# Output projection of an encoder: row blocks 8 to 11 kept in split form on chip and multiplied last, tile by tile

## The chip, the core and the metric

The kernel runs on one core of a Trainium2 chip, in one launch. The metric is the device time of that launch in microseconds (us). TensorE (PE in the profile, PEld for its weight loads), VectorE (DVE), ScalarE (ACT), GpSimd (POOL) and the queue of SyncE (SP), which issues all the DMAs here, each run their own list of instructions in order and meet only at semaphores.

## What is computed

Two encoder layers over 1024 tokens of 1024 values. Each layer projects its input to queries, keys, values and a gate, attends, and closes with the output projection and a LayerNorm. The change is in that closing part and in what surrounds it:

```python
D_MODEL = 1024; SEQ = 1024; DEPTH = 2; D_INNER = 2 * D_MODEL
for i in range(DEPTH):
    ...
    y = jnp.concatenate([o_mix, o_mem], axis=1).transpose(0, 2, 1, 3).reshape(b, L, D_INNER)
    y = y * jax.nn.silu(gate)
    branch = jnp.einsum('ble,ed->bld', y, w_out[i])
    x = layer_norm(ALPHA * x + branch, ln_g[i], ln_b[i])
```

## The kernel before

All matmuls are made in three parts. An operand is split into a high part (a cast by ACT, `split_hi`, `y_tile`) and a low part (source minus high part, by DVE, `split_lo`, `y_tile`), and PE adds high by high, high by low and low by high.

**Output projection.** The 2048 values of `y` are 16 row blocks e of 128. The 1024 tokens are two halves h of 512, each of 4 row tiles t of 128 tokens. For one half the output is 4 tiles by 2 column halves c: 8 PSUM banks b = 2t + c, all of them. A block therefore costs 8 x 3 = 24 matmuls of 128x512, and a layer 2 x 16 x 24 = 768. PE goes through the blocks outside and the banks inside; only the last two blocks of a half are interleaved (`last_two`, lead 5). All eight banks of a half so end close together.

**Supply.** SP loads each weight piece (128x512, a *stage*) of `w_out` into `raw` (6 places) and each half block of `y` from `y_scratch` into `y_raw` (2 places). ACT and DVE split weights into `ring` (4 places, so two blocks) and `y` into `y_split` (2 places). A place is free when PE has ended the last matmul that reads it. In the order of the program all of them are 3 stages ahead of PE (`AHEAD`). Every weight piece is loaded and split twice, once for each half. The queue of SP also loads the residual rows (8 DMAs of 512 KB, one with each of the blocks 4 to 11 of the first half), `ln_g` and `ln_b`.

**After the matmuls.** DVE adds a bank to the residual (`add`), takes statistics for a tile (`statistics`), POOL turns them into a reciprocal deviation by four small operations, and `norm` scales and shifts: for tiles 0 to 3 DVE normalises and multiplies and POOL adds `b_row` over 1024 columns; for tiles 4 to 7 ACT normalises (L1521) and DVE does two operations of 1024 columns. Tiles 0 to 3 are normalised during blocks 4 to 7 of the second half, tiles 4 to 7 after its end. When layer 0 is closed, the rows are turned to columns for layer 1: `x_group` is four PE transposes (L1063) into a bank, a cast by ACT (L1306) and a subtraction by DVE; group 0 comes from the rows, others from sums of rows (`token_sums` and three more, DVE). Product 0 of layer 1 (12 matmuls) needs all four pieces of group 0, product 1 needs group 1, and PE transposes group 2 ahead of product 1.

## Time and profile before

| | us |
|---|---|
| median of 3 runs | 2169.07 (2167.77 to 2170.2) |
| the profiled execution, its own time | 2170.46 |
| its span, first to last instruction | 2168.6 |
| PE busy in the span | 2107.2 (97%) |
| DVE busy | 1628.4 (75%) |
| ACT busy | 1091.1 (50%) |
| mean granted TensorE clock | 0.99 |

PE is busy for 97% of the span, so a change can only win where PE stands still, or lose by making it do so. The page shows the span in 40 slices of 54 us; only slice 16 (813 to 867 us, the passage from layer 0 to layer 1: PE 5 tenths) and the last one are far from full. The output projections lie at 646 to 826 us and at 1973 to 2151 us.

### The profile page before, as it was taken

To read this page: it belongs to the slowest core of one execution; us is meant where nothing else is said; L and a number is where in the kernel's file an instruction comes from. 1 tells how busy PE (TensorE), PEld (TensorE's weight loads), DVE (VectorE), ACT (ScalarE), POOL (GpSimd) and SP (SyncE) were. 2 spreads that over 40 slices of the span, in tenths; PEclk is the share of its full clock that TensorE was granted. 3 is DMA by queue.
4 is the path that set the end of the run, shared out by engine and by line. 5 is a ranking of instruction groups with operands and counts; after the bars stand their busy time and mean duration, and the time that the engine had idled before them with its cause. 6 is when DMAs were issued, how large, how long until landed. Compare 5 with 4: busy or idle time off the path is not lost.

```text
span 2168.6 us, 31853 instructions
## 1 busy us (share of the span) xinstructions
PE 2107.2 (97%) x10880; PEld 1767.9 (82%) x10880; DVE 1628.4 (75%) x3673; ACT 1091.1 (50%) x2649; POOL 48.4 (2%) x65
## 2 busy tenths in 40 slices
PE   8999999999999995999999999999999999999996
PEld 8888888888888774888888888888888888888875
DVE  6777878787663568868888888888887888775485
ACT  5444444445553323455555555555555565564332
POOL 0000000000000021000000000000000000000031
PEclk9999999999999997999999999999999999999998
DMA  8311111111126542123233133133143233224643
GB/s 266 103 48 42 60 39 49 59 59 59 54 80 216 182 141 102 54 69 94 63 97 93 56 100 95 50 108 99 50 108 86 63 108 85 89 87 161 216 142 131
DMA packets 244619, 209.20 MB, mean 96 GB/s; under 512 B 21092, under 2 KB 198316, under 8 KB 244460
## 3 DMA queue, kind: packets, MB, share of 16 engines
q1 hardware_dynamic: 244460, 207.16, 31.8%
q8 instruction: 89, 1.46, 0.3%
q14 instruction: 70, 0.57, 0.1%
HBM read 172.60 MB, written 34.52 MB: 96 GB/s over the span
## 4 chain that ended last, share of the span: by engine, by line
PE 78%; DVE 13%; DMA 5%; issue 2%; ACT 2%; SPq 0%; DVEq 0%; ACTq 0%
PE bank L1086 15%; PE bank L1084 15%; PE bank L1085 15%; PE bank L1162 8%; PE bank L1134 7%; DVE work L1536 5%; PE bank L1256 4%; PE bank L1260 4%; PE bank L1262 4%; PE bank L1148 4%; DVE ring L1536 2%; DMA work<-weight_scratch 1%; DMA weight_scratch<-trig 1%; DVE x_ops L1536 1%; PE bank L1063 1%
## 5 line engine op out<-in xcount | busy, mean ns | idle before, releaser
L1084 PE MATMUL bank<-x_ops,ring 128*128 128x512 f32 (+1 forms) x1808 | 844.5, 467 | 16.9 <-issue 14.8
L1086 PE MATMUL bank<-x_ops,ring 128*128 128x512 f32 (+1 forms) x1808 | 698.9, 387 | 0.0
L1085 PE MATMUL bank<-x_ops,ring 128*128 128x512 f32 (+1 forms) x1808 | 697.0, 386 | 0.0
L1536 DVE SCALAR_TENSOR_TENSOR ring<-raw,ring 128x512 fp32r<-128x512 f32 x400 | 272.9, 684 | 232.9 <-ACT ring L1302 232.6
L1086 PEld LDWEIGHTS bank<-x_ops,ring 128*128 128x128 f32 x1808 | 341.0, 189 | 71.3
L1084 PEld LDWEIGHTS bank<-x_ops,ring 128*128 128x128 f32 x1808 | 345.7, 191 | 61.4 <-issue 15.5
L1363 ACT COPY work<-bank 128x256 f32<-128x256 f32 (+2 forms) x448 | 164.3, 367 | 430.1 <-PE bank L1148 429.3
L1085 PEld LDWEIGHTS bank<-x_ops,ring 128*128 128x128 f32 x1808 | 345.5, 191 | 37.5
L1302 ACT CAST ring<-raw 128x512 fp32r<-128x512 f32 x400 | 246.5, 618 | 198.4 <-PE bank L1262 173.0
L1162 PEld LDWEIGHTS bank<-work 128*128 128x128 f32 x1744 | 262.2, 190 | 44.4 <-ACT work L1363 3.9
L1380 ACT ACTIVATE work<-work,soft 128x256 f32<-128x256 f32 (+2 forms) x448 | 226.5, 506 | 134.3 <-DVE soft L1680 132.6
L1134 PE MATMUL bank<-work 128*128 128x256 f32 (+2 forms) x896 | 267.2, 380 | 3.0 <-DVE soft L1680 3.0
L1162 PE MATMUL bank<-work 128*128 128x128 f32 x1744 | 267.6, 275 | 2.5 <-ACT work L1363 1.2
L1536 DVE SCALAR_TENSOR_TENSOR work<-work 128x512 f32<-128x512 f32 (+4 forms) x352 | 233.3, 678 | 34.5 <-DMA work<-weight_scratch 31.5
L1134 PEld LDWEIGHTS bank<-work 128*128 128x128 f32 x896 | 183.3, 215 | 39.9 <-DVE soft L1680 7.8
L1536 DVE SCALAR_TENSOR_TENSOR work<-work,trig 32x512 f32<-32x512 f32 x304 | 207.2, 710 | 0.8
L1256 PE MATMUL bank<-ring,x_ops 128*128 128x512 f32 x512 | 200.4, 391 | 6.9 <-DVE x_ops L1536 5.3
L1262 PE MATMUL bank<-ring,x_ops 128*128 128x512 f32 x512 | 199.3, 389 | 0.0
L1260 PE MATMUL bank<-ring,x_ops 128*128 128x512 f32 x512 | 199.3, 389 | 0.0
L1536 DVE SCALAR_TENSOR_TENSOR ring<-sums,ring 128x512 fp32r<-128x512 f32 x180 | 123.0, 683 | 68.2 <-ACT ring L1302 68.1
L1148 PE MATMUL bank<-ident,work 128*128 128x128 f32 x872 | 168.7, 273 | 0.5 <-DVE work L1690 0.5
L1148 PEld LDWEIGHTS bank<-ident,work 128*128 128x128 f32 x872 | 114.2, 140 | 34.9 <-ACT work L1380 4.5
(74 smaller groups left out, 2020.8 us busy)
## 6 DMA issues: line engine op xcount, KB each, us to landing
raw<-in_w_in_b SPq DMA_DIRECT2D x160, 256.0 KB, 3.1
raw<-in_w_out SPq DMA_DIRECT2D x128, 256.0 KB, 2.9
raw<-in_w_in_a SPq DMA_DIRECT2D x80, 256.0 KB, 3.0
work<-weight_scratch SPq DMA_DIRECT2D x24, 768.0 KB, 5.2
y_scratch<-work SPq DMA_DIRECT2D x32, 512.0 KB, 2.8
x_ops<-y_scratch SPq DMA_DIRECT2D x64, 256.0 KB, 3.7
work<-v_scratch SPq DMA_DIRECT2D x48, 256.0 KB, 4.4
raw<-in_w_mkv SPq DMA_DIRECT2D x32, 256.0 KB, 5.1
```

The lines of the kernel that those rows point to most:

```text
L1084: nc.tensor.matmul(dst, w_h, x_h, start=start, stop=False, skip_group_check=again)
L1085: nc.tensor.matmul(dst, w_h, x_l, start=False, stop=False, skip_group_check=again)
L1086: return nc.tensor.matmul(dst, w_l, x_h, start=False, stop=stop, skip_group_check=again)
L1134: nc.tensor.matmul(SB[count % 2][:, 0:size], q, k, start=True, stop=True).then_inc(s_ready, 1)
L1148: mm = nc.tensor.transpose(TB[x_n % 2][:, c * P:(c + 1) * P], p[:, k0:k0 + P], ident[:, :])
L1162: mm = nc.tensor.matmul(dst, job.values(v), pT[layer][count % 2][:, c * P:(c + 1) * P], start=(c == 0), stop=(c == len(chunks) - 1))
L1256: mm = nc.tensor.matmul(BB[b][:, :], y_h, ring[:, n % RING, 0, :], start=first, stop=False)
L1260: nc.tensor.matmul(BB[b][:, :], y_h, ring[:, n % RING, 1, :], start=False, stop=False)
L1262: mm = nc.tensor.matmul(BB[b][:, :], y_l, ring[:, n % RING, 0, :], start=False, stop=last)
L1302: nc.scalar.copy(ring[:, n % RING, 0, :], src).then_inc(w_hi, 1)
L1380: nc.scalar.activation(p_view(layer, count % 3, size, sink), s_view(layer, count % 3, size, sink), ACT.Exp, bias=low[:, job.stat, t:t + 1] ...
L1536: return nc.vector.scalar_tensor_tensor(out=dst, in0=a, scalar=1.0, in1=b, op0=ALU.mult, op1=op)
```

## The change

Row blocks 8 to 11 are called LATE, the other twelve EARLY; the *place* of an early block is its index among these. In the first half, after the stages of the early blocks at places 1, 4, 7 and 10, the two weight stages of one late block are loaded and split, not into the ring but into `late`, and stay there for both halves. The `y` of the late blocks goes to four more places of `y_split`, in both halves. Stages of a layer fall from 64 to 56. PE multiplies the early blocks as before and the late ones at the end of a half, tile by tile: for tile 0 all four late blocks, then tile 1, and so on. `add` and `statistics` stand together for each tile. In the second half `norm` of tiles 4 to 6 stands between them, and in layer 0 group 0 of the columns and the first sums of rows do too. The bigger `y_split` and `late` take memory that products 2 to 5 of the last pair read, so the first two loads of `y` wait for product 3 and not for product 2. Residual rows are loaded at places 5 to 8 of the first half and at places 1 to 4 of the second, `ln_g` and `ln_b` at places 10 and 11.

```diff
-OUT_STAGES = 4 * NE
+
+
+EARLY = (0, 1, 2, 3, 4, 5, 6, 7, 12, 13, 14, 15)
+LATE = (8, 9, 10, 11)
+
+
+
+OUT_ORDER = []
+for half in range(2):
+    for place, block in enumerate(EARLY):
+        OUT_ORDER += [(half, block, 0), (half, block, 1)]
+        if half == 0 and place % 3 == 1:
+            OUT_ORDER += [(0, LATE[place // 3], 0), (0, LATE[place // 3], 1)]
+OUT_STAGES = len(OUT_ORDER)
+Y_ORDER = [(half, block) for half in range(2) for place, early in enumerate(EARLY)
+           for block in ((early, LATE[place // 3]) if place % 3 == 1 else (early,))]
...
+        Y_SLOTS = 2 + len(LATE)
+        y_split = x_ops[:, 2 * XW:2 * XW + 1024 * Y_SLOTS].rearrange("p (s a n) -> p s a n",
+                                                                     s=Y_SLOTS, a=2)
+        y_raw = x_ops[:, 4 * XW - 1024:4 * XW].bitcast(F32).rearrange("p (s n) -> p s n", s=2)
+        late = x_ops[:, 4 * XW:6 * XW].rearrange("p (s a n) -> p s a n", s=2 * len(LATE), a=2)
...
-        XB = bank[4:8]
+        XB = (bank[4:8], bank[2:6])
...
-                    ((0,), (1, 2), (3,), (4,), (5, 6), (), ()))
+                    ((), (1, 2), (3,), (4,), (5, 6), (), ()))
...
+        def y_events(m):
+
+            h, e, c = OUT_ORDER[m]
+            if c == 0 or e in LATE:
+                return []
+            place = EARLY.index(e)
+            blocks = (e, LATE[place // 3]) if place % 3 == 1 else (e,)
+            return [Y_ORDER.index((h, block)) for block in blocks]
...
+                return OUT_STAGE[out_piece(n)[0]] - 1
+            k = ring_no[n] - RING
+            return ring_stages[k] if k >= 0 else None
...
+        def y_slot(e):
+            return 2 + LATE.index(e) if e in LATE else EARLY.index(e) % 2
...
-                    if T == products(layer) - 15:
-                        sp.wait_ge(*product_done(FIRST_PAIR[layer] + PAIRS[layer] - 1, 2))
-                        for e in range(2):
-                            load_y_of(layer)(0, e)
+                    if T == products(layer) - 11:
+                        sp.wait_ge(*product_done(FIRST_PAIR[layer] + PAIRS[layer] - 1, 3))
+                        for q in range(2):
+                            load_y(layer, q)
...
+            def load_y(layer, q):
+                h, e = Y_ORDER[q]
+                if q >= 2:
+                    sp.wait_ge(y_lo, layer * 2 * NE + q - 1)
+                if h == 0:
+                    sp.wait_ge(*store_done[layer, e])
+                nc.sync.dma_start(y_raw[:, q % 2, :], y_dram[e, :, h * HALF:(h + 1) * HALF]
...
-                        q = h * NE + e + 2
-                        if q < 2 * NE:
-                            load_y(q // NE, q % NE)
-                        loads_after(n + 1 + AHEAD)
+                for m in range(AHEAD, OUT_STAGES + AHEAD):
+                    loads_after(OUT_STAGE[layer] + m)
+                    if m >= OUT_STAGES:
+                        continue
+                    h, e, c = OUT_ORDER[m]
+                    if c == 1 and e in EARLY:
+                        place = EARLY.index(e)
+                        if h == 0 and 5 <= place < 9:
+                            load_residual(layer, residual, place - 5)
+                        if h == 0 and place >= 10:
+                            load_norm(layer, place - 10)
+                        if h == 1 and 1 <= place < 5:
+                            load_residual(layer, residual, 3 + place)
+                    for q in y_events(m):
+                        if q + 1 < 2 * NE:
+                            load_y(layer, q + 1)
...
-                    pe.wait_ge(z_free, 8 + BRANCH_BANKS.index(4 + i) + 1)
+                    pe.wait_ge(z_free, 8 + BRANCH_BANKS.index(2 + i) + 1)
...
-                def last_two(h):
-                    lead = 5
-                    is_split(h, NE - 2)
-                    for b in range(lead):
-                        add_to(h, NE - 2, b)
-                    is_split(h, NE - 1)
-                    for b in range(8):
-                        add_to(h, NE - 1, b, last=True)
-                        if b + lead < 8:
-                            add_to(h, NE - 2, b + lead, ends=b + lead >= 6)
-
                 for h in range(2):
-                    for e in range(NE - 2):
+                    for e in EARLY:
                         is_split(h, e)
                         for b in range(8):
-                            add_to(h, e, b, first=e == 0, ends=b >= 6)
-                    last_two(h)
+                            add_to(h, e, b, first=e == EARLY[0], ends=b >= 6)
+                    for t in range(4):
+                        for e in LATE:
+                            if t == 0:
+                                is_split(h, e)
+                            for c in range(2):
+                                add_to(h, e, 2 * t + c, last=e == LATE[-1])
+                        if layer == 0 and h == 1 and t >= 2:
+                            for i in ((0, 1, 2), (3,))[t - 2]:
+                                x_group(1, 0, i)
...
+                elif e in LATE:
+                    act.wait_ge(*((br_ready, layer * 16 + 8) if h else finished(OUT_STAGE[layer] - 1)))
+                elif (h, e) not in ((0, EARLY[0]), (0, EARLY[1])):
+                    place = h * len(EARLY) + EARLY.index(e) - 2
+                    act.wait_ge(*finished(out_stage(layer, place // len(EARLY),
+                                                    EARLY[place % len(EARLY)], 1)))
+                nc.scalar.copy(y_split[:, y_slot(e), 0, :], y_raw[:, slot, :]).then_inc(y_hi, 1)
...
-                for q in range(2 * NE):
-                    n = OUT_STAGE[layer] + 2 * q
-                    if n + AHEAD < STAGES:
-                        split_hi(n + AHEAD)
-                    if q + 1 < 2 * NE:
-                        y_tile(layer, q + 1)
-                    if n + 1 + AHEAD < STAGES:
-                        split_hi(n + 1 + AHEAD)
+                for m in range(AHEAD, OUT_STAGES + AHEAD):
+                    if OUT_STAGE[layer] + m < STAGES:
+                        split_hi(OUT_STAGE[layer] + m)
+                    for q in y_events(m) if m < OUT_STAGES else ():
+                        y_tile(layer, q)
                 for t in range(4, TILES):
+                    if layer == 0 and t == 6:
+                        for i in range(3):
+                            x_group(1, 0, i)
                     act.wait_ge(ln_mean, 2 * (layer * 4 + t - 3))
                     nc.scalar.activation(rows[:, t, :], rows[:, t, :], ACT.Identity,
                                          bias=rstd[:, t, 0:1], scale=rstd[:, t, 1:2]
                                          ).then_inc(ln_normal[1], 1)
+                if layer == 0:
+                    x_group(1, 0, 3)
...
+                        for op in X_BEFORE[layer][T // 4]:
+                            for i in range(4):
+                                x_group(layer, op, i)
                         if layer == 1 and T in (4, 8):
                             for i in range(4):
                                 (third_token_sums, fourth_token_sums)[T // 4 - 1](1, i)
-                        for op in X_BEFORE[layer][T // 4]:
-                            for i in range(4):
-                                x_group(layer, op, i)
-                        if layer == 1 and T == 0:
-                            for i in range(4):
-                                token_sums(1, i)
-                                second_token_sums(1, i)
...
-                for q in range(NE - 1):
-                    stage_pair(q)
-                n = OUT_STAGE[layer] + 2 * NE - 2
-                for b in range(3):
-                    add(0, b)
-                y_tile(layer, NE)
-                split_lo(n + AHEAD)
-                for b in range(3, 7):
-                    add(0, b)
-                split_lo(n + 1 + AHEAD)
-                add(0, 7)
-                for q in range(NE, 2 * NE - 1):
-                    stage_pair(q)
-                    if q < NE + 4:
-                        statistics(q - NE)
-                    elif q < NE + 8:
-                        norm(q - NE - 4)
-                n = OUT_STAGE[layer] + 4 * NE - 2
-                for b in range(8):
-                    add(1, b)
-                    if b % 2 == 1:
-                        statistics(4 + b // 2)
-                    if b == 2 and n + AHEAD < STAGES:
-                        split_lo(n + AHEAD)
-                if n + 1 + AHEAD < STAGES:
-                    split_lo(n + 1 + AHEAD)
+                second = 2 * NE + AHEAD
+                for m in range(AHEAD, second):
+                    stage(m)
+                for t in range(4):
+                    add(0, 2 * t)
+                    add(0, 2 * t + 1)
+                    statistics(t)
+                for m in range(second, OUT_STAGES + AHEAD):
+                    stage(m)
+                    if m in range(second + 8, second + 16, 2):
+                        norm((m - second - 8) // 2)
+                if layer == 0:
                     third_sum(FIRST_PAIR[1])
                     fourth_sum(FIRST_PAIR[1])
-                for t in range(4, TILES):
-                    norm(t)
+                for i in range(4):
+                    add(1, 2 * i)
+                    add(1, 2 * i + 1)
+                    statistics(4 + i)
+                    if layer == 0 and i == 3:
+                        for k in range(3):
+                            x_group(1, 0, k)
+                    if i > 0:
+                        norm(3 + i)
+                        if layer == 0:
+                            token_sums(1, i - 1)
+                            second_token_sums(1, i - 1)
+                if layer == 0:
+                    x_group(1, 0, 3)
+                norm(7)
+                if layer == 0:
+                    token_sums(1, 3)
+                    second_token_sums(1, 3)
```

ACT's list near the start of layer 0's output projection. `raw` to `ring` is a weight stage, `x_ops` from `x_ops` is a tile of `y`, `x_ops` from `raw` a stage kept in `late`. Before:

```order
L1302 CAST ring<-raw 128x512 [waits prod,raw_in1]
L1439 CAST x_ops<-x_ops 128x512 [waits y_full1]
L1302 CAST ring<-raw 128x512 [waits prod,raw_in2]
L1302 CAST ring<-raw 128x512 [waits prod,raw_in3]
L1439 CAST x_ops<-x_ops 128x512 [waits prod,y_full0]
```

Now:

```order
L1353 CAST ring<-raw 128x512 [waits prod,raw_in1]
L1494 CAST x_ops<-x_ops 128x512 [waits y_full1]
L1494 CAST x_ops<-x_ops 128x512 [waits prod,y_full0]
L1353 CAST x_ops<-raw 128x512 [waits prod,raw_in2]
L1353 CAST x_ops<-raw 128x512 [waits prod,raw_in3]
L1353 CAST ring<-raw 128x512 [waits prod,raw_in4]
L1353 CAST ring<-raw 128x512 [waits prod,raw_in5]
L1494 CAST x_ops<-x_ops 128x512 [waits prod,y_full1]
```

The late block's `y` comes right behind the early one's, and the next block's three casts come behind the late block's.

DVE's list in the second half of layer 0, where tiles 1 to 3 are normalised (a `TENSOR_SCALAR` and the `work<-work` behind it are one `norm`). Before:

```order
L1896 TENSOR_SCALAR work<-work 128x1024
L1536 SCALAR_TENSOR_TENSOR work<-work 128x1024
L1536 SCALAR_TENSOR_TENSOR ring<-raw,ring 128x512
L1536 SCALAR_TENSOR_TENSOR x_ops<-x_ops 128x512
L1536 SCALAR_TENSOR_TENSOR ring<-raw,ring 128x512
L1896 TENSOR_SCALAR work<-work 128x1024
L1536 SCALAR_TENSOR_TENSOR work<-work 128x1024
```

Now:

```order
L1946 TENSOR_SCALAR work<-work 128x1024
L1593 SCALAR_TENSOR_TENSOR work<-work 128x1024
L1593 SCALAR_TENSOR_TENSOR ring<-raw,ring 128x512 x2
L1593 SCALAR_TENSOR_TENSOR x_ops<-x_ops 128x512 x2
L1946 TENSOR_SCALAR work<-work 128x1024
L1593 SCALAR_TENSOR_TENSOR work<-work 128x1024
L1593 SCALAR_TENSOR_TENSOR ring<-raw,ring 128x512 x2
L1593 SCALAR_TENSOR_TENSOR x_ops<-x_ops 128x512
```

A `norm` now stands behind the `y` of its block and not between the two stages, and at place 7 it stands behind two tiles of `y`, the second of them late block 10.

DVE's list from layer 0 to layer 1, from the last two tiles on. Before:

```order
L1878 SCALAR_TENSOR_TENSOR work<-work,bank 128x512 x2
L1886 BN_STATS work<-work 128x6 x2
L1889 BN_AGGR work<-work 128x2
L1536 SCALAR_TENSOR_TENSOR ring<-sums,ring 128x512
L1536 SCALAR_TENSOR_TENSOR raw<-raw 128x512
L1536 SCALAR_TENSOR_TENSOR sums<-raw,sums 128x512
L1536 SCALAR_TENSOR_TENSOR work<-work 128x1024 x8
L1536 SCALAR_TENSOR_TENSOR x_ops<-bank,x_ops 128x4x128 x4
L1536 SCALAR_TENSOR_TENSOR work<-work 128x512 x8
```

Now:

```order
L1928 SCALAR_TENSOR_TENSOR work<-work,bank 128x512 x2
L1936 BN_STATS work<-work 128x6 x2
L1939 BN_AGGR work<-work 128x2
L1593 SCALAR_TENSOR_TENSOR x_ops<-bank,x_ops 128x4x128 x3
L1593 SCALAR_TENSOR_TENSOR work<-work 128x1024 x2
L1593 SCALAR_TENSOR_TENSOR work<-work 128x512 x2
L1593 SCALAR_TENSOR_TENSOR x_ops<-bank,x_ops 128x4x128
L1593 SCALAR_TENSOR_TENSOR work<-work 128x1024 x2
L1593 SCALAR_TENSOR_TENSOR work<-work 128x512 x2
```

Behind the last statistics four operations of 1024 columns and four of 512 remain where there were eight and eight, and the columns stand ahead of them.

## Rows read from the trace of the kernel before

**Rows 1.** Busy time by stretch: us, busy of each engine (x), PEclk, DMA share, GB/s

```profile
646.00:826.00 180.00, 175.88 (x768) 143.53 (x768) 95.10 (x134) 57.53 (x95) 16.84 (x13) 1.00 0.56 183
840.00:850.00 10.00, 0.97 (x2) 0.83 (x3) 9.86 (x12) 1.87 (x4) 0.00 (x0) 0.50 0.52 210
860.00:865.00 5.00, 5.00 (x20) 4.07 (x19) 4.91 (x9) 2.15 (x4) 0.00 (x0) 0.66 0.04 11
```

**Rows 2.** Timeline of PE, layer 0: start us, us, engine, line, what [idle before]

```profile
646.45 0.47 PE L1256 MATMUL bank<-ring,x_ops 128*128 128x512 f32 x1 [1.45 <-issue]
725.68 0.39 PE L1260 MATMUL bank<-ring,x_ops 128*128 128x512 f32 x1
725.91 0.39 PE L1262 MATMUL bank<-ring,x_ops 128*128 128x512 f32 x1
727.86 0.47 PE L1256 MATMUL bank<-ring,x_ops 128*128 128x512 f32 x1 [1.56 <-DVE x_ops L1536]
...
768.04 0.39 PE L1262 MATMUL bank<-ring,x_ops 128*128 128x512 f32 x1
769.29 0.47 PE L1256 MATMUL bank<-ring,x_ops 128*128 128x512 f32 x1 [0.86 <-DVE x_ops L1536]
```

**Rows 3.** Timeline of DVE, one norm of layer 0's second half

```profile
763.06 0.69 DVE L1536 SCALAR_TENSOR_TENSOR ring<-raw,ring 128x512 fp32r<-128x512 f32 x1 [2.15 <-ACT ring L1302]
763.66 0.81 DVE L1896 TENSOR_SCALAR work<-work 128x1024 f32<-128x1024 f32 x1
764.51 1.23 DVE L1536 SCALAR_TENSOR_TENSOR work<-work 128x1024 f32<-128x1024 f32 x1
765.65 0.68 DVE L1536 SCALAR_TENSOR_TENSOR ring<-raw,ring 128x512 fp32r<-128x512 f32 x1
766.25 2.89 DVE L1536 SCALAR_TENSOR_TENSOR x_ops<-x_ops 128x512 fp32r<-128x512 f32 x1
```

**Rows 4.** Timeline of POOL at the same norm

```profile
765.82 2.78 POOL L1044 TENSOR_TENSOR work<-work 128x1024 f32<-128x1024 f32 x1 [4.50 <-DVE work L1536]
```

**Rows 5.** Timelines of SP and ACT: loads of y and the casts that wait

```profile
650.69 0.59 SPq L962 DMA_DIRECT2D x_ops<-y_scratch  x1
...
654.81 0.62 ACT L1439 CAST x_ops<-x_ops 128x512 fp32r<-128x512 f32 x1 [1.91 <-DMA x_ops<-y_scratch]
...
670.87 0.38 SPq L962 DMA_DIRECT2D x_ops<-y_scratch  x1
...
1981.88 0.62 ACT L1439 CAST x_ops<-x_ops 128x512 fp32r<-128x512 f32 x1 [2.49 <-DMA x_ops<-y_scratch]
...
1997.45 0.38 SPq L962 DMA_DIRECT2D x_ops<-y_scratch  x1
...
2002.75 0.62 ACT L1439 CAST x_ops<-x_ops 128x512 fp32r<-128x512 f32 x1 [1.60 <-DMA x_ops<-y_scratch]
```

**Rows 6.** The y loads of line L962, all 64: from issue to landing

```profile
DMA to landing us min/median/max: 2.7/3.7/6.2
```

**Rows 7.** Timeline of PE from layer 0 to layer 1

```profile
825.27 0.39 PE L1262 MATMUL bank<-ring,x_ops 128*128 128x512 f32 x1
...
849.03 0.76 PE L1084 MATMUL bank<-x_ops,ring 128*128 128x512 f32 x1 [14.82 <-issue]
...
861.14 0.78 PE L1084 MATMUL bank<-x_ops,ring 128*128 128x512 f32 x1
```

**Rows 8.** Timeline of DVE from layer 0 to layer 1

```profile
836.86 9.67 DVE L1536 SCALAR_TENSOR_TENSOR work<-work 128x1024 f32<-128x1024 f32 x8
846.46 2.48 DVE L1536 SCALAR_TENSOR_TENSOR x_ops<-bank,x_ops 128x512 fp32r<-128x512 f32 x4
848.85 5.40 DVE L1536 SCALAR_TENSOR_TENSOR work<-work 128x512 f32<-128x512 f32 x8
```

**Rows 9.** Timelines at the end of the kernel: PE, DVE and POOL

```profile
2150.66 0.39 PE L1262 MATMUL bank<-ring,x_ops 128*128 128x512 f32 x1
...
2155.98 9.62 DVE L1536 SCALAR_TENSOR_TENSOR work<-work 128x1024 f32<-128x1024 f32 x8
...
2157.29 1.54 POOL L1032 TENSOR_TENSOR work<-work,power 128x1 f32<-128x1 f32 x1
```

145 lines of the change are left out of this document (65 added, 80 removed).

## The prediction

> **What bounds the kernel now.** I read the stretches first, then the gaps between PE's instructions, then DVE, POOL and ACT around each gap. PE is busy 175.88 of the 180 us of layer 0's output projection, at a granted clock of 1.00 [rows 1]. Its matmuls start 0.227 us apart (725.68 and 725.91, to two digits [rows 2]), so a block of 24 takes 5.44 us and 768 take 174.1 us. From 646.45 to the end of the last one (825.27 + 0.23 = 825.50) are 179.05 us [rows 2, 7]. Of the 5.0 us lost, 1.7 stand at 725.91 to 727.86, where block 15's y is late, and 1.0 at 768.04 to 769.29; three more gaps behind three more norms take 0.45 each, so 4.1 are stalls. Layer 1 has the same norm gaps and 0.7 elsewhere: 3.1. The two big holes lie outside. Layer 1's product 0 starts at 849.03, product 1 at 861.14, that is 23.5 and 35.6 us after the last matmul of layer 0 [rows 7], while DVE works through eight norm operations, four column pieces and eight sums without a pause [rows 8]. At the end the span goes on for 17.7 us after the last matmul (2150.66 + 0.23 to 2168.6), 9.6 of them the same eight norm operations [rows 9].
>
> **The passage to layer 1.** Let E be when PE would end the last half without other work. Three groups of transposes now stand ahead of the last tile: 12 transposes, 1.25 us (16 took 1.67 between two products), so its last matmul ends at T = E + 1.25. The tiles end 5.44 us apart. DVE needs for one tile 2 adds (0.6 each), statistics (1.5), a norm (2.4: eight operations took 9.67) and two sums (1.35: eight took 5.40) [rows 8], 6.45 us, so it falls behind by 1 us a tile and stands about T + 0.3 when the last tile ends. Then: adds and statistics to T + 3.0, three column pieces (0.62 each) to 4.8, norm 6 to 7.2, sums to 8.55, the fourth column piece to 9.2. That piece waits for ACT, whose cast stands behind its normalising of tile 7, itself behind POOL's four small operations; they took 1.4 to 4.7 us, so it can be T + 10.2. Product 0 starts at T + 9.8. PE has then stood for over 9 us. In the old hole the granted clock was 0.50 [rows 1], the lower of its two levels, 1.2 GHz, and product 0 took 4.9 us for 12 matmuls; I take that again, to T + 14.7. Norm 7 and the last sums end at T + 13.6, under it. Product 1 waited 7.2 us behind product 0, partly because DVE made four sums before the column pieces. With the pieces first: first cast 0.8 after product 0, four casts, the last subtraction at 3.6, four transposes, 4.2 us. Product 1 so starts at T + 18.9 = E + 20.15, against 35.6. Gain **15.5 us**. Between 13 (a late fourth piece, sums that push group 3) and 17 (product 1 at full clock).
>
> **The end of the kernel.** DVE has no backlog now (5.1 us of work for a tile). Last adds and statistics to E + 2.4. POOL's four operations run beside norm 6; one of them took 1.54 us beside the norms [rows 9], all four 4.7, where 1.4 is normal. Here DVE is free again at E + 5.3, so POOL ends by about 5.5, ACT by 6.75, norm 7 by 9.2, and the store adds 3.0 as now. That is 12.2 against 17.7: gain **5.5 us**, between 4.5 and 7.1 (POOL undisturbed).
>
> **The late blocks' y.** This is what the change adds. Let s be the start of a block on PE. What the block after it needs (two stages, one y) is split in a burst: casts at s - 0.3, + 0.35 and + 0.9, the second stage's low part done at s + 1.7, y's at + 2.3. SP issues the load of the next y only behind the load that waits for that second stage: at s + 2.2, with a residual DMA between at s + 2.7 (670.87 with s = 646.45 + 4 x 5.44 = 668.2 [rows 2, 5]). Today that y has four microseconds until its cast is due. For a late block the cast is next in ACT's list, and the next early block's casts stand behind it. Landing, by the casts that waited: 4.1 us without a residual (650.69 to 654.81) and 5.3 with one (1997.45 to 2002.75; sixteen such are 4.0 to 6.2, mostly 5.0 to 5.6), the least and the median of all 64 being 2.7 and 3.7 [rows 5, 6]. I take 3.7 and 5.2. The Trainium skill (DMA: Bandwidth & Descriptors, Rules for kernel authors) says to issue a DMA early and wait on its semaphore late. Its fit in Anatomy of one DMA, about 2.0 us plus bytes at 436 GB/s, would as an estimate give 2.6 us for a y of 256 KB, and the time would come out near 2159; the measured 3.7 and 5.2 decide.
>
> From the cast of the late y at t, DVE ends the next early block's y at t + 4.35 in the first half (six operations in a row, 0.6 each) and t + 3.15 in the second (four). It is due at s + 10.9.
> - *First half, start:* the cast waits until 654.81 in layer 0 and 1981.88 in layer 1 [rows 5]; block 2 is ready at 659.2 and 1986.3, due 657.3 and 1983.9. Stall 2.0 and 2.4.
> - *Place 4:* t = s + 5.9, no stall. But the next y is loaded only behind the burst's last stage (s + 9.65), with a residual between: lands s + 15.85, ready 17.2, due 16.3. Stall 0.95.
> - *Place 7:* t = s + 2.7 + 5.2 = 7.9, ready 12.2: 1.45, and the next y 1.4 by the same chain. *Place 10,* behind `ln_g`: 1.45.
> - *Second half, place 1:* with M the start of the half, DVE has add, statistics, stage and y until M + 3.6; the load is issued at 4.0, t = 9.2, ready 12.4, due 10.9: 1.6 with the hand-over, the next y 1.4. Place 4: 0.3. Place 10: none, with t = s + 5.9 and four operations.
>
> **The norms.** POOL's add over 1024 columns takes 2.78 us, and a DVE operation that started beside it took 2.89 instead of 0.69, ending 0.54 after it [rows 3, 4]. A norm at n so ends the second operation behind it at n + 5.5, and four of them make DVE, not PE, set the pace: 6.0 us a block. Before, this cost 1.0 + 3 x 0.45. Now the norm stands behind the y, which spares nothing, since place 4's late burst has used up DVE's lead by then: 0.6, 0.55 and 0.55 at places 5, 6 and 8. At place 7 late block 10's y is ahead of the norm. Its load waits for the second stage, which POOL holds until s + 5.3: issued 5.7, cast 9.4, DVE done 10.7; only then norm 2 to 12.7, a stage, a stage held to 16.15, y to 16.75. The block was due at 11.45. Stall **5.4 us**. After so long a stand I add 0.7 a layer for a lower clock, which the slack of the next norm covers in part; the row for it is product 1, whose 5 us from 860 on had a mean granted clock of 0.66 behind a stand of PE of 2.8 us [rows 1].
>
> **Sum.** Layer 0: 2.0 + 0.95 + 1.45 + 1.4 + 1.45 + 1.6 + 1.4 + 0.3 + 1.7 + 5.4 + 0.7 = 18.35, less 4.1 = 14.25. Layer 1: 18.75 - 3.1 = 15.65. Together +29.9, against -15.5 and -5.5: **+8.9 us**. The profiled execution would go from a span of 2168.6 to 2177.5 and from 2170.46 to 2179.4; it lies 1.4 above the median of the runs, so the median goes from 2169.07 to 2178.0. Other edits are free: 8 weight loads and 8 pairs of splits fewer a layer, since PE waits for the order and not for the amount; y's first loads four steps later, some 5 us, for data that lies ready longer than that (if it did not, the whole half would start late by the rest). The late matmuls read another memory than the ring, at the same price.
>
> **The rivals.** *Same (2167):* the loads land at the fast ends, 3.2 and 4.3 us. Then place 4 and most of the residual stalls go, place 7 costs 5.0, and the additions are 19.2, less 21.0. For it: three of the sixteen at 4.0 to 4.3. Against: two y loads now follow each other and the first half carries its loads in 65 us instead of 87. *Faster (2157):* loads of y that land in 2.7 us, the least [rows 6], take away all but the start, the norms and 4.3 us at place 7: additions 10.6, so 2159. Or, at 3.2 and 4.3, DVE keeps a lead of 2 us or more into the norms. It decides at place 7: if the second stage is split before POOL starts, late block 10 costs 1.8 and not 5.4 a layer (-7), and product 1 and the end take their best values (-3). Against it, DVE's full 6.0 us a block leaves nothing to regain. *Slower still (2193):* landings of 4.1 and 6.2 make the additions 42 and the passage gives 2 less or so; a first half at 0.74 DMA share speaks for it a little. *Not as it says (2186):* ACT's cast of tile 7 or the fourth column piece holds product 0 so that half of the passage's gain is lost.
>
> **How the numbers follow.** Forecast 0.50, same 0.20, faster 0.15, slower still 0.10, not as it says 0.05. A measurement of this kernel tells 0.2%, 4.3 us, from no change. The faster case and a little of the same case give 0.20 for faster; the rest of that case and the low end of the forecast's own range (2171 to 2187) give 0.20 for the same; 0.60 for slower. The range, 2158 to 2192, leaves out about half of the faster and half of the slowest case.
>
> **What would show it.** Right: in each second half one gap of about 5 us in PE before the block at place 8, with a late cast and a norm in front; gaps of 1 to 2 us behind the bursts at places 1, 4, 7 and 10; casts of late y that wait 3 to 6 us for a DMA; product 1 about 20 us after E; a store 12 us after the last matmul. Wrong: output projections of 180 us or less, or a passage above 25 us. The single largest doubt is the landing time of y, which enters most of the stalls.

## The result: 2187.8 us, 0.8% slower

The changed kernel takes 2187.82 us (median of 4 runs, 2185.93 to 2190.91). The kernel before took 2169.21 beside it, so the ratio is 1.0082, with a 95% interval of 1.007 to 1.0094. The forecast was slower by 8.9 us; it is slower by 18.6. The profiled execution took 2188.07 us, its span is 2186.3, so 17.7 above the span before.

I cut both spans at the same five points. A projection runs from its first matmul to the end of its last one; in layer 0 the 1.2 us of the twelve transposes are taken out of it and put to the passage.

| us | before | after | difference | forecast |
|---|---|---|---|---|
| until layer 0's projection | 646.45 | 646.02 | -0.4 | 0 |
| its matmuls | 179.05 | 195.94 | +16.9 | +14.25 |
| passage, to layer 1's product 1 | 35.64 | 20.86 | -14.8 | -15.5 |
| body of layer 1, to its projection | 1111.8 | 1116.4 | +4.6 | 0 |
| layer 1's projection | 177.95 | 194.52 | +16.6 | +15.65 |
| from the last matmul to the end | 17.71 | 12.59 | -5.1 | -5.5 |
| sum | | | +17.7 | +8.9 |

The stretch of layer 0's projection, by windows (us, busy of PE, PEld, DVE, ACT and POOL with counts, PEclk, DMA share, GB/s). It answers to the first row of [rows 1]: 699 matmuls instead of 768 fit in, and the clock is no longer full. The second row is the body.

```profile
646.00:826.00 180.00, 166.51 (x699) 134.52 (x700) 88.77 (x126) 50.04 (x88) 14.27 (x12) 0.96 0.51 171
862.82:1979.19 1116.37, 1107.53 (x5807) 933.34 (x5805) 917.72 (x2212) 630.49 (x1671) 0.31 (x1) 1.00 0.30 83
```

The biggest stall stands in each second half. PE's timeline after the change (start us, us, engine, line, operation, idle before and its releaser):

```profile
790.43 0.39 PE L1316 MATMUL bank<-ring,x_ops 128*128 128x512 f32 x1
795.20 0.76 PE L1314 MATMUL bank<-ring,x_ops 128*128 128x512 f32 x1 [4.38 <-DVE x_ops L1593]
795.76 0.63 PE L1315 MATMUL bank<-ring,x_ops 128*128 128x512 f32 x1
...
800.02 0.63 PE L1316 MATMUL bank<-ring,x_ops 128*128 128x512 f32 x1
800.45 0.44 PE L1314 MATMUL bank<-ring,x_ops 128*128 128x512 f32 x1
```

What DVE, ACT, POOL and SP did ahead of it, from their timelines:

```profile
781.04 3.13 SPq L845 DMA_DIRECT2D raw<-in_w_out  x2
784.22 0.91 SPq L1020 DMA_DIRECT2D x_ops<-y_scratch  x2
...
787.77 0.62 ACT L1494 CAST x_ops<-x_ops 128x512 fp32r<-128x512 f32 x1 [5.46 <-DMA x_ops<-y_scratch]
...
788.42 0.69 DVE L1593 SCALAR_TENSOR_TENSOR x_ops<-x_ops 128x512 fp32r<-128x512 f32 x1 [4.00 <-ACT x_ops L1494]
789.03 0.81 DVE L1946 TENSOR_SCALAR work<-work 128x1024 f32<-128x1024 f32 x1
789.88 1.23 DVE L1593 SCALAR_TENSOR_TENSOR work<-work 128x1024 f32<-128x1024 f32 x1
791.02 3.43 DVE L1593 SCALAR_TENSOR_TENSOR ring<-raw,ring 128x512 fp32r<-128x512 f32 x2
791.18 2.72 POOL L1105 TENSOR_TENSOR work<-work 128x1024 f32<-128x1024 f32 x1 [7.91 <-DVE work L1593]
794.37 0.68 DVE L1593 SCALAR_TENSOR_TENSOR x_ops<-x_ops 128x512 fp32r<-128x512 f32 x1
```

It is the chain of the forecast: SP issues late block 10's y at 784.2 only, its cast waits for the landing until 787.8, DVE is idle 4.0 us for it, then norm 2 comes, POOL's add holds DVE, and the y of the next block is split at 795. PE stops 4.5 us (forecast 5.4). The 12 matmuls behind the stop start 0.43 us apart and not 0.227, which is the granted clock at the lower of its two levels, 1.2 GHz:

```profile
795.20:800.40 5.20, 5.20 (x12) 4.09 (x13) 5.17 (x5) 0.62 (x1) 2.75 (x1) 0.50 0.46 151
```

The y loads of line L1020, all 64, against 2.7/3.7/6.2 in [rows 6], and who waited for them, us and times:

```profile
  ACT x_ops L1494: 203.8, 38
...
DMA to landing us min/median/max: 2.5/4.8/7.9
```

The passage, on PE and DVE, against [rows 7, 8]. Its last matmul before ends at 843.19:

```profile
843.85 1.28 DVE L1928 SCALAR_TENSOR_TENSOR work<-work,bank 128x512 f32<-128x512 f32 x2
...
846.61 1.83 DVE L1593 SCALAR_TENSOR_TENSOR x_ops<-bank,x_ops 128x512 fp32r<-128x512 f32 x3
848.36 4.00 DVE L1593 SCALAR_TENSOR_TENSOR work<-work 128x1024 f32<-128x1024 f32 x4
852.27 0.68 DVE L1593 SCALAR_TENSOR_TENSOR x_ops<-bank,x_ops 128x512 fp32r<-128x512 f32 x1
...
853.05 0.77 PE L1144 MATMUL bank<-x_ops,ring 128*128 128x512 f32 x1 [9.27 <-issue]
...
862.82 0.48 PE L1144 MATMUL bank<-x_ops,ring 128*128 128x512 f32 x1
```

And the end of the kernel, DVE and POOL behind the last matmul's end at 2173.71, against [rows 9]:

```profile
2176.08 2.44 DVE L1593 SCALAR_TENSOR_TENSOR work<-work 128x1024 f32<-128x1024 f32 x2
...
2177.38 1.54 POOL L1093 TENSOR_TENSOR work<-work,power 128x1 f32<-128x1 f32 x1
...
2180.76 2.48 DVE L1593 SCALAR_TENSOR_TENSOR work<-work 128x1024 f32<-128x1024 f32 x2 [2.25 <-ACT work L1576]
```

### The profile page after: what moved, and what is told of

It is laid out like the page before. It is cut to its first block, busy times and chain, and to the rows that moved or that the text cites. A ratio compares the mean times of both kernels' runs of the same rounds, so it can differ in the third digit from the quotient of the medians.

```text
span 2186.3 us, 31789 instructions
## 1 busy us (share of the span) xinstructions
PE 2117.8 (97%) x10880; PEld 1772.1 (81%) x10880; DVE 1614.7 (74%) x3657; ACT 1073.8 (49%) x2633; POOL 49.4 (2%) x65
## 4 chain that ended last, share of the span: by engine, by line
PE 64%; DVE 17%; DMA 11%; issue 3%; ACT 2%; SPq 2%; POOL 0%; DVEq 0%; ACTq 0%; POOLq 0%
PE bank L1144 13%; PE bank L1146 13%; PE bank L1145 13%; PE bank L1222 7%; PE bank L1194 6%; DVE work L1593 6%; DMA x_ops<-y_scratch 4%; DVE ring L1593 4%; PE bank L1208 3%; PE bank L1314 3%; PE bank L1316 3%; PE bank L1315 3%; DMA work<-weight_scratch 2%; DMA weight_scratch<-trig 2%; DVE x_ops L1593 2%
## 5 line engine op out<-in xcount | busy, mean ns | idle before, releaser
L1593 DVE SCALAR_TENSOR_TENSOR ring<-raw,ring 128x512 fp32r<-128x512 f32 x368 | 265.3, 729 | 115.8 <-ACT ring L1353 115.5
L1593 DVE SCALAR_TENSOR_TENSOR work<-work 128x512 f32<-128x512 f32 (+4 forms) x352 | 233.8, 677 | 42.6 <-DMA work<-weight_scratch 36.8
L1353 ACT CAST ring<-raw 128x512 fp32r<-128x512 f32 x368 | 223.9, 616 | 41.7 <-PE bank L1316 24.1
L1314 PE MATMUL bank<-ring,x_ops 128*128 128x512 f32 x384 | 155.3, 404 | 29.4 <-DVE x_ops L1593 27.8
L1315 PE MATMUL bank<-ring,x_ops 128*128 128x512 f32 x384 | 152.9, 398 | 0.0
L1316 PE MATMUL bank<-ring,x_ops 128*128 128x512 f32 x384 | 152.8, 398 | 0.0
L1593 DVE SCALAR_TENSOR_TENSOR x_ops<-x_ops 128x512 fp32r<-128x512 f32 x64 | 43.9, 687 | 136.8 <-ACT x_ops L1494 136.8
```

The source lines that it names most:

```text
L1314: nc.tensor.matmul(BB[b][:, :], y[:, 0], w[:, 0, :], start=first, stop=False)
L1315: nc.tensor.matmul(BB[b][:, :], y[:, 0], w[:, 1, :], start=False, stop=False)
L1316: mm = nc.tensor.matmul(BB[b][:, :], y[:, 1], w[:, 0, :], start=False, stop=last)
L1353: nc.scalar.copy(split_slot(n)[:, 0, :], src).then_inc(w_hi, 1)
L1593: return nc.vector.scalar_tensor_tensor(out=dst, in0=a, scalar=1.0, in1=b, op0=ALU.mult, op1=op)
```

## The experiments

Two questions were open: what makes the projections longer (the landing of y, DVE's norms, or both), and why a body that the change doesn't touch is 4.6 us longer. "Stops" below are places where two matmuls of a projection start over 0.55 us apart, less the 0.23 that one takes; "slow steps" is the time lost in those that start 0.3 to 0.55 us apart. Projections of layer 0 are given without the transposes.

### Norms apart

```
-                    if m in range(second + 8, second + 16, 2):
-                        norm((m - second - 8) // 2)
+                    if m - second in (8, 10, 14, 16):
+                        norm((8, 10, 14, 16).index(m - second))
```

> Edit: VectorE's norms 0 to 3 of the first half stand at second-half stages 8, 10, 14 and 16 instead of 8, 10, 12 and 14, so none stands between late block 10's y tile and the stages of place 7. Theory (the three norms in a row, with the y tile behind them, hold VectorE too long and TensorE waits 4.8 to 5.3 us at place 7 and then runs some ten matmuls at the lower clock): the gap before place 7 shrinks from 4.8 us (layer 0) and 5.3 us (layer 1) to under 2.5 us, at most half of it reappears a place later, and the kernel takes 2 to 5 us less a layer, 2178 to 2184 us. Rival (the gap is the y load's landing behind a residual load, norms or not): the gaps stay within 1 us of what they are and the time stays at 2187 to 2189 us.

Measured: 2176.95 us, ratio to before 1.0029 (1.0016 to 1.0042), some 11 us below the changed kernel. In layer 0 the stop of 4.5 us has become three of 0.4 and one of 0.9; the projections take 190.6 and 190.8 us. The norm at place 7 is a cause. The gain is a little above what I had named (up to 10 us): in the profiles the projections give 9.1 us, and the body, which the edit doesn't touch, is 2.7 us shorter. Layer 0's slow steps fell from 6.3 to 2.5 us, but two later profiles of the changed kernel, nothing edited, have only 1.9 and 2.0, so that fall is not shown to be the edit's.

### The y loads three tiles ahead

```
-        y_raw = x_ops[:, 4 * XW - 1024:4 * XW].bitcast(F32).rearrange("p (s n) -> p s n", s=2)
+        y_raw = x_ops[:, 4 * XW - 2048:4 * XW].bitcast(F32).rearrange("p (s n) -> p s n", s=4)
...
-                        for q in range(2):
+                        for q in range(4):
...
-                        if q + 1 < 2 * NE:
-                            load_y(layer, q + 1)
+                        if q + 3 < 2 * NE:
+                            load_y(layer, q + 3)
```

> Edit: four buffers for the raw y tiles instead of two (in space that is free), and each y tile's load issued three y tiles ahead instead of one. Nothing else moves. Theory (the out projections are longer because a y load is issued only when the y tile before it is split, and the late blocks' tiles stand right behind an early one's, so TensorE waits out a DMA's landing): the TensorE gaps after places 1, 4, 7 and 10 of each half that end on a y tile vanish, 7 to 9 us a layer with 1 to 2 us of lower clock behind them; the gaps of the norms stay or halve. Layer 0's projection falls from 195.9 us to 184 to 188, layer 1's likewise, the kernel takes 2166 to 2174 us. Rival (VectorE and ScalarE are too full in these stretches, so the landing only stands where their work would): the gaps stay in sum within 3 us of 16 us a layer and the time is 2182 to 2188 us.

Measured: 2141.94 us, ratio 0.987 (0.9853 to 0.9886). That is 46 us below the changed kernel and 28 below the kernel before. The same stretch as above, by windows, with more matmuls (the transposes among them) than ever, and the clock is full:

```profile
646.00:826.00 180.00, 176.40 (x784) 145.75 (x784) 106.15 (x154) 56.14 (x95) 22.33 (x24) 1.00 0.52 175
```

The projections take 174.6 and 174.5 us, which is 768 matmuls at 0.227 us and nothing else. The landing itself is as slow as in the changed kernel, and no cast waited for it in either layer:

```profile
DMA to landing us min/median/max: 2.9/4.8/7.4
```

The theory was right in kind, but its gain (14 to 22 us) was less than half of the 46: I had left the norms' stops in. They vanish too. A norm holds DVE for some 5 us, and DVE now has a lead to pay that from: it was idle for 2.9, 1.5, 0.7 and 0 us ahead of the stages in front of the four norms of layer 0. So the lead is just used up when the norms are over.

### Both

> Both edits: four raw y buffers with loads three ahead, and norms 0 to 3 at second-half stages 8, 10, 14 and 16. Theory: both kinds of stall are gone, each projection takes 179 to 184 us (its matmuls alone took about 176 to 178 in the kernel before), and with the shorter passage (14.8 us) and tail (5.1 us) the kernel takes 2154 to 2164 us, under the kernel before at 2169. Rival (VectorE is the bound in the second half, whatever the order): each projection stays above 186 us and the kernel takes 2170 us or more.

Measured: 2140.87 us, ratio 0.9865 (0.985 to 0.9879), projections of 174.3 and 174.2 us. Below the expected range, and no different from early loads alone. This is the version to keep, with or without the norms moved.

### Raw slots of layer 1 as in the kernel before

```
+def slot_of(load):
+    return (load + (SHIFT if load >= LAYER_LOAD[1] else 0)) % RAW
```

> Edit: the changed kernel with layer 1's raw weight loads put in the slots that they have in the kernel before (shifted by two of six), since 56 out-projection loads a layer instead of 64 change which of the six raw buffers each load of layer 1 uses. Nothing else moves. Theory A (layer 1's body, from its second product to its out projection, takes 1116.4 us instead of 1111.8 because the slots' phase against the pairs changed): the body falls to 1112 to 1113 us and the kernel takes 2182 to 2185 us. Theory B (the body's length has nothing to do with the slots: the moment at which it starts and DMA jitter in the softmax exchange make it): the body stays at 1115 to 1118 us or varies from run to run without regard to the slots, and the time is 2187 to 2189 us.

(The rest of the edit puts `slot_of` in place of `load % RAW`.) Measured: 2186.09 us, ratio 1.0075 (1.0059 to 1.009), between the two theories' ranges. The body took 1111.9 us, as theory A says, but layer 1's projection 197.3 us. One profile cannot tell; more profiles of kernels with and without this shift are below.

### The kernel before with early y loads

```
-                        for e in range(2):
+                        for e in range(4):
...
-                        q = h * NE + e + 2
+                        q = h * NE + e + 4
```

> Edit, of the kernel before: four raw y buffers instead of two and each y load issued four tiles ahead of its place instead of two; the order of the output projection stays as it was. Theory (early y loads take away only the stalls on y tiles, and what the order with late blocks brings is a thing apart): the projections fall from 179.1 and 178.0 us to the 175 us that 768 matmuls take at the full clock, and the kernel takes 2160 to 2164 us; then the changed order with early loads, at 2142 us, is worth 18 to 22 us, the 14.8 us of the passage and 5.1 us of the tail that the trace showed. Rival (the early loads shorten something else, such as the body of layer 1): the kernel takes under 2155 us.

Measured: 2166.82 us, ratio 0.9979 (0.997 to 0.9989). That is above the expected range. The projections take 177.0 us each, not 175: the norms' stops stay here (2.4 us a projection), which I had not expected, although no cast waited for a y. In this order a norm stands between the two stages of a block, and POOL's add holds the y behind it (2.88 us), as DVE's timeline of this kernel shows:

```profile
767.84 0.80 DVE L1896 TENSOR_SCALAR work<-work 128x1024 f32<-128x1024 f32 x1
768.67 1.23 DVE L1536 SCALAR_TENSOR_TENSOR work<-work 128x1024 f32<-128x1024 f32 x1
769.81 0.68 DVE L1536 SCALAR_TENSOR_TENSOR ring<-raw,ring 128x512 fp32r<-128x512 f32 x1
770.42 2.88 DVE L1536 SCALAR_TENSOR_TENSOR x_ops<-x_ops 128x512 fp32r<-128x512 f32 x1
```

In the changed order a norm stands behind the block's stages and y. The prediction said that this "spares nothing"; with early loads it goes with no stop at all. Early loads are worth 4 us to the order of before and 46 us to the changed one. Between the two kernels with early loads lie 24.9 us. In their profiled executions, 22.9 us apart, the passage gives 15.1, the end 5.1, the projections 4.9, and the body takes back 2.2.

### Residual loads behind the y loads

Only the two blocks of statements in SP's loop change places, so that the y load of a stage is issued ahead of its residual load.

```
+                    for q in y_events(m):
+                        if q + 1 < 2 * NE:
+                            load_y(layer, q + 1)
                     if c == 1 and e in EARLY:
...
-                    for q in y_events(m):
-                        if q + 1 < 2 * NE:
-                            load_y(layer, q + 1)
```

> Edit, of the changed kernel: at a stage that issues both a residual load (512 KB) and a y load, the y load is issued first. Theory (a y load behind a residual load lands 1.5 us later than a plain one, and three to five of these in a layer end on the path): the y loads' landing falls by about 1 to 2 us there, each projection by 2 to 5 us, and the kernel takes 2178 to 2184 us. Rival (the load's place in the row of weight loads sets its landing, not the residual): the projections stay within 1.5 us of 194 to 196 us and the time is 2186 to 2189 us.

Measured: 2166.68 us, ratio 0.9983 (0.9974 to 0.9992). A swap of two DMAs' order is worth 21 us, about as much as all that the change costs. The first residual load of layer 0 and the y load beside it, from SP's timeline, and the cast that waited for that y, from ACT's, in the changed kernel:

```profile
672.37 2.13 SPq L845 DMA_DIRECT2D raw<-in_w_out  x4
674.61 0.36 SPq L1030 DMA_DIRECT2D work<-in_x  x1
675.07 0.38 SPq L1020 DMA_DIRECT2D x_ops<-y_scratch  x1
...
681.55 0.62 ACT L1494 CAST x_ops<-x_ops 128x512 fp32r<-128x512 f32 x1 [5.38 <-DMA x_ops<-y_scratch]
```

and with the order swapped:

```profile
672.35 2.13 SPq L845 DMA_DIRECT2D raw<-in_w_out  x4
674.58 0.38 SPq L1020 DMA_DIRECT2D x_ops<-y_scratch  x1
675.06 0.36 SPq L1030 DMA_DIRECT2D work<-in_x  x1
...
679.22 0.62 ACT L1494 CAST x_ops<-x_ops 128x512 fp32r<-128x512 f32 x1 [2.68 <-DMA x_ops<-y_scratch]
```

The y is there 6.5 us after its issue in one case, 4.6 in the other. In front of it SP has issued four weight loads (1 MB) and a residual (512 KB) within 2.7 us, and all of them land in the order of issue, y last. The residual adds 1.8 us to this landing, where I had taken 1.5. A layer has ten stages with such a pair (eight residual loads, two of the norm's rows), and its projection fell by 10.3 and 9.4 us, to 185.7 and 185.2: I had put the stalls that hang on a residual far too low, at some 1.5 us each for three to five of them. Place 7's stop stayed (5.1 and 4.4 us), as it hangs on the norm.

### The y loads two tiles ahead, and four buffers with the loads where they were

```
-                        if q + 3 < 2 * NE:
-                            load_y(layer, q + 3)
+                        if q + 2 < 2 * NE:
+                            load_y(layer, q + 2)
```

> Edit, of the changed kernel: four raw y buffers, y loads two tiles ahead instead of one (three ahead gave 2142 us). Theory (the pair of an early and a late tile at places 1, 4, 7 and 10 needs just one more load in flight): nearly all of the gain is there, 2142 to 2150 us. Rival (loads that stand at the pair's own stage still come too late): half of the gain, 2155 to 2170 us.

Measured: 2144.36 us, ratio 0.9877 (0.9862 to 0.9892). One load more in flight is nearly all of it. The second kernel of the pair has the same four buffers and `q + 1`:

> Edit, of the changed kernel: four raw y buffers, but each y load issued where it was, one tile ahead. Theory (what counts is the place of the load in the order in which SyncE issues, not the buffer that it waits for: its waits on the split tile are 2.9 us in all in layer 0's projection): the time stays at 2185 to 2189 us. Rival (SyncE held at the buffer's wait delays the load): 2 to 3 us a layer less, 2180 to 2184 us, or more if it is what made the gaps.

Measured: 2185.61 us, ratio 1.0065 (1.005 to 1.008), as the theory says. The buffers alone do nothing. It is the place of the load among SP's instructions that matters.

### Norms apart and residual loads behind; and all three edits

> Edit, of the changed kernel: norms 0 to 3 at second-half stages 8, 10, 14 and 16, and each y load ahead of the residual load of its stage; y loads still one tile ahead and two raw buffers. Theory (norms in a row and residual loads ahead of y loads are two separate causes of stall: alone they gave about 11 and 21 us): together about 28 to 32 us, 2156 to 2160 us, each projection 181 to 184 us. Rival (they share the same stalls): 2163 to 2167 us, no better than the residual loads alone.

Measured: 2156.48 us (2155.49 to 2164.25), ratio 0.9943 (0.9921 to 0.9965). The two gains add: projections of 182.0 and 181.5 us. With the early loads as well:

> Edit, of the changed kernel: four raw y buffers with loads three ahead, norms at stages 8, 10, 14 and 16, and y loads ahead of residual loads. Theory (with loads three ahead no y tile is late any more, so nothing is left for the other two edits to remove): the same as loads three ahead alone, 2139 to 2142 us, projections at 174 to 176 us. Rival (stalls are still hidden in the averages): 2137 us or less.

Measured: 2142.52 us, ratio 0.9871 (0.9856 to 0.9885). Nothing was left to remove.

### Transposes behind the last matmul

```
-                        if layer == 0 and h == 1 and t >= 2:
-                            for i in ((0, 1, 2), (3,))[t - 2]:
+                        if layer == 0 and h == 1 and t == 3:
+                            for i in range(4):
                                 x_group(1, 0, i)
```

> Edit, of the kernel with early y loads and norms apart: the transposes of layer 1's first three groups stand behind the last matmul of layer 0's projection instead of ahead of the last row tile's 24 matmuls; VectorE's and ScalarE's orders stay. Theory A (the passage is set by VectorE, which only gets to these groups 3.4 us after the last matmul, behind the last adds and statistics): the last matmul comes 1.2 us earlier, product 0 stands 9 to 10 us behind it as before, and the kernel is 0 to 1.5 us faster, 2139 to 2141 us. Theory B (the transposes made early are part of the passage's gain): product 0 comes 11 us or more after the last matmul and the kernel takes 2142 to 2145 us.

Measured: 2143.49 us (2139.59 to 2146.13), ratio 0.9874 (0.9856 to 0.9892). Theory B's two numbers came true (product 0 stands 11.2 us behind the last matmul), but not what it says, that the early transposes are part of the gain. Counted from the start of the projection, the last matmul ended 1.3 us earlier (174.2 against 175.5 us), but product 0 came at the same time: 831.76 - 646.35 = 185.41 us, against 831.19 - 645.77 = 185.42 with the transposes ahead. DVE has no pause here with either order and begins the adds of the last tile 176.2 us after the start in both: its backlog of statistics and norms from the tiles before sets when it reaches that tile, not PE. The early transposes do not bring product 0 forward. The medians, 2143.49 and 2140.87 us, have overlapping intervals and don't tell the two apart.

### The same kernels once more

> The changed kernel, nothing edited, profiled once more. Layer 1's body took 1116.4 us in its first profile; kernels with the same body have since shown 1109.8 to 1115.7 us, and the kernel with shifted slots 1111.9. Theory B (the body's length varies from execution to execution): a body at 1110 to 1115 us this time, with the projections again at 194 to 198 us, the passage at 19 to 20 us and a tail of 12.6 us, in all 2183 to 2188 us. Rival (this kernel's start of the body makes it 1116 us each time): 1116 to 1117 us again.

Measured: 2184.53 us, ratio 1.0059 (1.0039 to 1.0078). Projections 193.0 and 195.7 us, passage and end as in its first profile, body 1117.7: this goes with the rival. The same kernel was 2187.8 us in its first measurement, so the gains over it given above may be some 3 us smaller.

> The kernel before, nothing edited, profiled once more; its body took 1111.8 us. Theory B (the body's length varies from execution to execution, mostly in the eleven waits for the exchanged softmax weights): it comes out anywhere from 1110 to 1120 us, more than 1 us from 1111.8. Rival (each kernel has its own length): 1111.3 to 1112.3 us again.

> The changed kernel, nothing edited, third profile; its body took 1116.4 and 1117.7 us. Theory B (the length varies by execution): as for the kernel before, and the two ranges overlap. Rival (the changed kernel's body is always longer): 1115.5 us or more again.

> The kernel with norms apart and y loads ahead of residual loads, second profile; its body took 1120.1 us in an execution of 2164 us, while others of it took 2155.5 us. Theory B: a body at least 3 us from 1120, most likely 1111 to 1116 us, with a time of 2155 to 2160 us. Rival (own length): 1119 to 1121 us.

> The kernel with early y loads and norms apart, second profile; its body took 1109.8 us. Theory B: 1110 to 1116 us, more than 1 us from 1109.8. Rival (own length, short where no y tile is late): 1109.3 to 1110.3 us.

The four took 2167.70, 2186.51, 2154.81 and 2140.18 us. Their bodies beside the earlier ones, and DVE's waits in them for the softmax weights that the heads exchange through DRAM (11 waits each):

| kernel | body, us | these waits, us |
|---|---|---|
| before, twice | 1111.8, 1109.7 | 31.5, 30.9 |
| changed, three times | 1116.4, 1117.7, 1116.1 | 36.8, 36.6, 36.4 |
| norms apart and residual behind, twice | 1120.1, 1111.0 | 37.0, 32.0 |
| early y loads, norms apart, twice | 1109.8, 1110.6 | 31.0, 31.4 |
| changed with four buffers only | 1111.0 | 32.1 |
| changed with shifted slots | 1111.9 | 32.8 |
| norms apart; residual loads behind | 1113.7; 1115.7 | 34.6; 35.9 |
| early y loads, in four other kernels | 1113.5, 1113.2, 1112.3, 1110.0 | 34.7, 33.5, 33.4, 30.9 |
| before with early y loads | 1111.3 | 33.0 |

One row of the list of waits for each of the two executions of the kernel with norms apart and residual loads behind (engine, line, what it waited for: us in total, times, longest):

```profile
DVE work L1593 <- DMA work<-weight_scratch: 37.0, 11, 4.2
```

```profile
DVE work L1593 <- DMA work<-weight_scratch: 32.0, 11, 4.0
```

Theory B holds in kind for two of the four (the kernel before moved by 2.1 us, to just below the range, the one with norms apart and residual loads behind by 9.1), the rival for the changed kernel; the last, 0.8 us off, speaks for neither. One kernel's body varies by 9 us, and with it these waits by 5. In 17 of the 18 profiles the body less these eleven waits is 1078.3 to 1081.1 us, in the longest one 1083.1: it is these waits that make a body long or short. The kernel with four buffers only has the changed kernel's slots and its late projections, and its body took 1111.0 us, so neither of these alone makes a body long. But the changed kernel was long three times of three and the kernel before short both times. Whether something in the changed kernel draws the exchange into its slower case stays open.

## Why the prediction was right in kind, and gave half of the size

**Passage and end, right.** Product 0 came 9.86 us after T (forecast 9.8), product 1 19.6 (18.9), the end 12.6 us after the last matmul (12.2). DVE took its last adds at T + 0.7 (forecast 0.3), and the forecast's reading, DVE behind by about 1 us a tile, fits the kernel with the transposes last, where DVE had no pause and reached the last tile at the same time. POOL had tile 7's four small operations done in 1.4 us, so the fourth column piece came at T + 9.1.

**The stalls on y and the norms, right in kind and nearly in sum.** Layer 0, the stops that the forecast named, with two profiles of the changed kernel:

| | forecast | first | second |
|---|---|---|---|
| start | 2.0 | 1.75 | 2.2 |
| place 4's next y | 0.95 | 2.3 | 1.5 |
| place 7, and its next y | 2.85 | 1.9 | 2.8 |
| place 10 | 1.45 | 0.8 | 1.5 |
| second half, place 1 and its next y | 3.0 | 3.2 | 2.5 |
| place 7 of the second half | 5.4 | 4.5 | 5.2 |
| norms and place 4 of the second half | 2.0 | 0.4 | 0.4 |
| slow steps | 0.7 | 6.3 | 1.9 |
| sum | 18.35 | 21.2 | 18.0 |

Over its three profiles layer 0's matmuls took 195.9, 193.0 and 192.7 us (forecast 193.3), layer 1's 194.5, 195.7 and 196.7 (193.6). The landing is the term on which these rest. The forecast took 3.7 us, and 5.2 behind a residual. Of the 64 y loads of the changed kernel, the 20 issued right behind a transfer of 512 KB landed in 6.0 us (median) and the other 44 in 4.4. That is near the 4.1 and 6.2 of the prediction's "slower still" rival, for which it worked out additions of 42 us; they were 33.5. So the chain from a landing to a stall was priced too high, and the landing too low, and that the two nearly cancel is luck. So is part of the sum in the table: the stops that were named came to 14.9 us in the first profile against 17.65, and the slow steps made up for it. The 2.6 us of the prediction's estimate from the Trainium skill (DMA: Bandwidth & Descriptors, Anatomy of one DMA) comes from a fit for DMAs that GpSimd issues, and these are issued by SyncE; here 2.5 us was the least and 4.8 the median. The Trainium skill (DMA: Bandwidth & Descriptors, Rules for kernel authors) asks for a DMA issued early and waited on late. Here the runs agree: two tiles ahead instead of one took 43 us off.

**Slow steps, too small.** I had 0.7 us a layer for the clock. The first profile shows 6.3 and 3.6, the second 1.9 and 3.9, the third 2.0 and 2.9. In the 18 profiles together, 13 stops of 4.1 to 5.2 us were each followed by 7 to 14 matmuls at half the pace, and of 21 stops of 2.0 to 2.8 us twelve by 8 or 9 of them and nine by none. No stop under 2 us was followed by such a row.

**The step that failed: the sum has nothing for the body of layer 1, and 0.7 us a layer for the clock.** "Other edits are free", it says, and lets the body alone. The body was 4.6 us longer in the profiled execution, half of the 8.8 us that the forecast lacks there, and 1117.7 and 1116.1 us in the two later profiles. The waits for the exchanged softmax weights account for it (36.8 us against 31.5); whether the change makes them longer stays open, as said above. The other term is the slow steps, 6.3 and 3.6 us where the sum has 0.7 each. The stops took back about half of that, so that the projections were 3.6 us longer than forecast. The passage and the end add 1.1, and the start takes 0.4 off. Measured again beside the kernel before, the changed kernel stood 13 to 16 us above it, and not 18.6, so some of the miss is scatter.

**The rivals.** "Same" and "faster" rested on y landing in 3.2 us or less, and in 4.3 or less behind a residual. It went the other way. At the first residual of layer 0, 1.5 MB now stand ahead of y (landing 6.5 us) where 1 MB stood before (5.5 us); that more bytes are the cause at every y is not shown. "Not as it says" names a time near the measured one, 2186 us, for a reason that did not occur: the passage kept its gain, 14.8 us. The order itself could have brought what "faster" said and more, had the loads been placed for it: 2141 us.

## What to carry to other kernels

When an order is changed so that two consumers follow each other at once, move the loads of the second one too: count how many loads must be in flight at the densest spot, not on average. Of the DMAs that a queue issues in one burst, put the one that is waited for first. Price a landing by the bytes that are issued shortly ahead of it, not by the median of the kernel before. Price a stall of TensorE of over 2 us by its length and some more for the clock behind it: here nothing or some 1.6 us behind 2.0 to 2.8 us, and 1.5 to 2.9 us behind 4.1 to 5.2.

## What the runs showed of the hardware

- The y load of 256 KB landed in 2.5 to 7.9 us in the changed kernel. Behind 1.5 MB issued in 2.7 us it took 6.5 us, behind 1 MB issued in 2.2 us 4.6, and in the kernel before, behind 1 MB issued in 1.6 us, 5.5.
- After PE had stopped 4.1 to 5.2 us, it ran 7 to 14 matmuls 0.43 us apart (granted clock 0.50 in the window above), then 0.23 again. The same stop, place 7 in layer 0, cost 12 such matmuls in one execution of the changed kernel and 7 in another, and of the 21 stops of 2.0 to 2.8 us nine cost none. Behind a stop of 2.5 us the lower clock did not come at once: behind the one at 761.73 five steps of 0.22 to 0.31 us came first, and the half pace began at 762.97, 1.2 us after it:

```profile
761.73 0.47 PE L1314 MATMUL bank<-ring,x_ops 128*128 128x512 f32 x1 [2.35 <-DVE x_ops L1593]
762.04 0.40 PE L1315 MATMUL bank<-ring,x_ops 128*128 128x512 f32 x1
...
762.97 0.58 PE L1316 MATMUL bank<-ring,x_ops 128*128 128x512 f32 x1
763.35 0.63 PE L1314 MATMUL bank<-ring,x_ops 128*128 128x512 f32 x1
```

- A round trip of 12 KB through DRAM and back as 768 KB, with DVE waiting, had a wait of 2.1 to 4.7 us a time (18 profiles), and the sum of eleven of them went from 30.9 to 37.0 us, with bodies of 1110 to 1120 us.
